# First expert's rows by products with 0/1 lists, second expert's by the gather, and an early choice for tiles 0 to 2

## The reference, cut to what matters

```
t = rms_norm(h, m_norm[layer])                       # (512, 1024)
g_logits = t @ w_group + b_group                     # 4 groups;  softmax, top 1
e_logits = t @ w_expert + b_expert                   # 16 experts, 4 to a group
# in the chosen group: top 2 of the 4 experts, weights from both softmaxes
for e in range(16):
    hdn = silu(t @ w_gate[e]) * (t @ w_up[e])        # 1024 -> 512
    y  += combine[:, e] * (hdn @ w_down[e])          # 512 -> 1024
h = h + y
```

## Time and profile before

| | |
|---|---|
| median of 3 runs | 1139.48 us (1138.67 to 1140.58) |
| the profiled execution | 1143.3 us, span 1141.5 us |
| TensorE busy | 1078.8 us (95%) |
| VectorE, ScalarE, GpSimd busy | 508.6, 282.6, 265.0 us |
| mean granted clock of TensorE | 0.980 |
| experts of layer 0, line 1843 | from 264.45 us |
| experts of layer 1, line 1843 | from 849.70 us |

### The profile page before, as it was taken

How to read it: one execution, slowest core, us unless ns; L and a number is a source line. 1 busy time by engine, 2 the same in 40 slices (tenths; PEclk the granted TensorE clock), 3 DMA queues, 4 the chain that set the end, 5 groups by cost and what they waited for, 6 DMA issues and landing times.

```text
span 1141.5 us, 17926 instructions
## 1 busy us (share of the span) xinstructions
PE 1078.8 (95%) x7469; PEld 647.0 (57%) x7469; DVE 508.6 (45%) x939; ACT 282.6 (25%) x461; POOL 265.0 (23%) x373
## 2 busy tenths in 40 slices
PE   6999999999999999996999999999989999999991
PEld 5688887874444433342788877777844444344430
DVE  3465237545533233326422357763355432343317
ACT  4442344320000000004232227763210000000012
POOL 1200012004333443123000013340023344433131
PEclk9899999999999999998999999999989999999996
DMA  9443311248999999998223210004279999999965
GB/s 322 127 146 112 106 38 74 110 186 331 402 422 421 422 423 423 423 418 288 102 75 111 79 69 1 2 1 166 71 263 415 419 421 421 422 423 423 423 230 198
DMA packets 68699, 283.24 MB, mean 248 GB/s; under 512 B 15048, under 2 KB 15216, under 8 KB 44064
## 3 DMA queue, kind: packets, MB, share of 16 engines
q1 hardware_dynamic: 47440, 239.32, 52.3%
q0 software_dynamic: 15232, 38.69, 9.4%
q10 hardware_dynamic: 5968, 4.40, 1.2%
HBM read 259.96 MB, written 22.41 MB: 247 GB/s over the span
## 4 chain that ended last, share of the span: by engine, by line
PE 81%; DVE 6%; DMA 4%; issue 4%; POOL 4%; ACT 1%; SPq 0%; POOLq 0%; DVEq 0%
PE ps L1843 41%; PE ps L1510 11%; PE ps L1512 10%; PE ps L1511 10%; DMA w_f<-in_m_w_up 2%; POOL xn_r L2295 1%; PE ps L1742 1%; DVE h L1384 1%; DMA xn<-output_table,pos 1%; PE ps L1520 1%; PE ps L1971 1%; DVE xn_r L1435 1%; POOL xn_r L2288 1%; PE ps L1654 1%; PE ps L1732 1%
## 5 line engine op out<-in xcount | busy, mean ns | idle before, releaser
L1843 PE MATMUL ps<-raw,s_f 128*32 128x256 f32 (+1 forms) x1536 | 175.8, 455 | 1.3 <-issue 0.7
L1843 PE MATMUL ps<-w_f,s_f 128*32 128x256 f32 (+1 forms) x1536 | 173.0, 451 | 2.6 <-issue 1.8
L1843 PE MATMUL ps<-xT_f,s_f 128*32 128x256 f32 (+1 forms) x1344 | 150.1, 451 | 0.4 <-DMA xT_f<-in_m_w_up 0.4
L1198 DVE TENSOR_TENSOR pad<-pad,ps 128x256 f32<-128x256 f32 x32 | 13.5, 421 | 296.6 <-ACT pad L790 296.6
L1843 PEld LDWEIGHTS ps<-raw,s_f 128*32 128x32 f32 (+1 forms) x1536 | 67.8, 119 | 103.5 <-issue 84.1
L1843 PEld LDWEIGHTS ps<-w_f,s_f 128*32 128x32 f32 (+1 forms) x1536 | 69.1, 119 | 95.4 <-issue 70.5
L1843 PEld LDWEIGHTS ps<-xT_f,s_f 128*32 128x32 f32 (+1 forms) x1344 | 59.7, 119 | 93.0 <-issue 74.0
L939 DVE SCALAR_TENSOR_TENSOR w_lo<-raw,gainT,w_hi 128x512 fp32r<-128x512 f32 x88 | 60.2, 746 | 105.3 <-ACT w_hi L594 105.3
L1208 DVE STREAM_TRANSPOSE s_f<-pad 32x128 f32<-32x128 f32 x256 | 103.0, 403 | 4.1
L1510 PE MATMUL ps<-w_hi,xT_hi 128*128 128x512 f32 x240 | 97.7, 407 | 5.9 <-DVE w_lo L939 2.9
L2252 POOL DMA_DIRECT2D output_table<-pad x60 | 33.7, 566 | 293.0 <-ACT pad L796 282.5
(11 more groups left out here) (299 smaller groups left out, 1470.8 us busy)
## 6 DMA issues: line engine op xcount, KB each, us to landing
raw<-in_m_w_down SPq DMA_DIRECT2D x28, 1024.0 KB
w_f<-in_m_w_down SPq DMA_DIRECT2D x28, 1024.0 KB
xT_f<-in_m_w_gate SPq DMA_DIRECT2D x26, 1024.0 KB
xT_f<-in_m_w_up SPq DMA_DIRECT2D x26, 1024.0 KB
raw<-in_m_w_gate SPq DMA_DIRECT2D x18, 1024.0 KB
raw<-in_m_w_up SPq DMA_DIRECT2D x18, 1024.0 KB
w_f<-in_m_w_gate SPq DMA_DIRECT2D x18, 1024.0 KB
w_f<-in_m_w_up SPq DMA_DIRECT2D x18, 1024.0 KB
```

Of the source, the lines that this page charges most:

```text
L1198: ve.tensor_tensor(hid2[:, 0:2 * P], sil2[:, 0:2 * P], ps[:, 0, 2 * P:4 * P], ALU.mult)
L1843: ins = te.matmul(ps[rows * n:rows * (n + 1), bank + kind, 0:width // parts], stationary(k, kind), weights(k, parts, n), start=k == 0, sto ...
```

## The change

It has four parts.

1. **Early choice.** The choice becomes a function `select(first, last)` of a range of tiles. VectorE does tiles 0 to 2 in `out_tiles`, between the logits of tile 2 and the last add; their ranks are multiplied by TensorE between the two halves of the last tile's logits. Tile 3 is chosen in `router`.
2. **First expert's rows by products.** From the ranks VectorE makes, for the first two experts only, 0/1 tables of token by row (`first_sel` in fp32, `second_sel` in bf16). TensorE multiplies `first_sel` by the normed rows in `xn`, eight products of 128x96 by 128x512 into two banks; VectorE and ScalarE copy a bank each to `x_0`, and TensorE transposes `x_0` as it did the gathered rows. `second_sel` is multiplied by the token numbers (eight products one column wide), and this list drives the whole-row gather, now of the second expert.
3. **What moves.** The lists of all experts, their transposition and the transposes of the second expert's rows are multiplied inside the first expert's `up`, which starts after the first half of its rows is copied. `overflow_places` stands ahead of `row_quarter_numbers` on VectorE. `x_first` is gone; `x_half` copies halves of either expert. The quarter gathers of the second expert are gone.
4. **The stream.** `load_down` of the first expert (pair 4) is issued ahead of the wait for the gather, which is now the second expert's. Pair 6, into `xn`, also waits for the first expert's wide products.

```
 class scratch:   -free = [6144]   +free = [11264]     (tables of the choice; the others stay at 6144)
+x_0 = pad[0:CAP, 0:D]
+index_1 = sb("index_1", [P, CAP])
+id_parts = sb("id_parts", [P, 2, NT], BF16)
...
 sync, load_pair:
                 if p == OWN:
                     sp.wait_ge(A["rows_stored"], 16 * NT * (layer + 1))
+                    sp.wait_ge(E["x_tr"], 6 * layer + 2)
 sync, step:
+                    load_down(layer, p + 2, e - 1, g)
                     if isinstance(e, int) and e == 1:
-                        sp.wait_ge(E["x_loaded0"], x_loads(layer, 0, -1))
-                    load_down(layer, p + 2, e - 1, g)
+                        sp.wait_ge(E["x_loaded1"], x_loads(layer, 1, -1))
...
 scalar, out_tiles:
                 rows_out(j)
+                act.wait_ge(E["x_tr"], 6 * layer + 2)
+                se.copy(x_0[:, BN:D], ps[0:CAP, 5, :]).then_inc(A["router_exp"], 1)
...
 vector:
+            def places_of(sel, e, first, last):
+                return tt(sel[:, first:last, :], index_1[:, :].unsqueeze(1).broadcast_to([P, last - first, CAP]),
+                          rank_of_first[:, first:last, e:e + 1].broadcast_to([P, last - first, CAP]), ALU.is_equal)
+            def ranks_in(layer, first, last):
+                dve.wait_ge(M["ranks_done"], 2 * layer + (1 if first == 0 else 2))
+                link(stt(rank_of_first[:, first:last, :], ps[:, 6, 0:NT * NE].rearrange("p (i e) -> p i e", e=NE)[:, first:last, 0:2], 1.0,
+                         sel_b[:, first:last, 0:2], ALU.add, ALU.mult))
 vector, out_tiles:
                 times_gain(0)
-                logits_in(j - 1)
+                link(logits_in(j - 1))
+                select(0, j)
                 add(j, 1)
+                ranks_in(layer, 0, j)
+                places_of(first_sel, 0, 0, j).then_inc(V["places_ready"], 1)
                 dve.wait_ge(M["hT_tr"], (NT + 1) * (layer + 1))
 vector, at the start, ahead of gainT's copy:
+            dve.wait_ge(G["consts"], 2)
+            ve.tensor_copy(id_parts[:, :, :], token_id[:, :, 0:NT])
 vector, router, ahead of the lists of all experts:
+                select(last, NT)
+                places_of(second_sel, 1, 0, last)
+                ranks_in(layer, last, NT)
+                places_of(first_sel, 0, last, NT).then_inc(V["places_ready"], 1)
+                places_of(second_sel, 1, last, NT).then_inc(V["places_ready"], 1)
+                dve.wait_ge(E["x_tr"], 6 * layer + 1)
+                ve.tensor_copy(x_0[:, 0:BN], ps[0:CAP, 4, :]).then_inc(V["places_ready"], 1)
...
+                dve.wait_ge(M["lists_done"], 4 * layer + 1)
+                ve.tensor_copy(token_now[:, 1:2], ps[0:CAP, 2, 2 * P:2 * P + 1]).then_inc(V["tokens_ready"], 1)
+                for f in (0, 1):
+                    x_half(layer, 0, f).then_inc(E["x_in"], 1)
 vector, experts:
+                overflow_places(layer)
                 row_quarter_numbers(layer)
-                x_first(layer)
-                overflow_places(layer)
+                x_half(layer, 1, 0)
+                x_half(layer, 1, 1).then_inc(E["x_in"], 1)
...
 tensor, out_proj:
                 logits(last, range(BK))
+                ranks(layer, range(last))
                 h_transposed_to(last, range(BK, KT))
+                pe.wait_ge(V["places_ready"], 6 * layer + 1)
+                pe.wait_ge(V["xn_ready"], NT * layer + last)
+                first_rows(0, 0)
                 logits(last, range(BK, KT))
+            def first_rows(t, n):
+                return te.matmul(ps[0:CAP, 4 + n, :], first_sel[:, t, :], xn[:, t, BN * n:BN * (n + 1)],
+                                 start=t == 0, stop=t == NT - 1, skip_group_check=True)
 tensor, router (kept_warm(3), the ranks of all tiles, kept_warm(1) and lists(...) go):
+                for t, n in ((0, 1), (1, 0), (1, 1), (2, 0), (2, 1)):
+                    first_rows(t, n)
+                ranks(layer, range(last, NT))
+                kept_warm(1)
+                pe.wait_ge(V["places_ready"], 6 * layer + 2)
+                pe.wait_ge(A["xn_scaled"], layer + 1)
+                for n in (0, 1):
+                    first_rows(last, n).then_inc(E["x_tr"], 1)
+                pe.wait_ge(V["places_ready"], 6 * layer + 3)
+                for t in range(NT):
+                    for c in range(2):
+                        ins = te.matmul(ps[0:CAP, 2, 2 * P:2 * P + 1], second_sel[:, t, :], id_parts[:, c, t:t + 1],
+                                        start=t + c == 0, stop=t + c == NT)
+                ins.then_inc(M["lists_done"], 1)
+                kept_warm(1)
+                pe.wait_ge(V["places_ready"], 6 * layer + 4)
+                pe.wait_ge(A["router_exp"], 3 * layer + 1)
+                x_transposed(E, x_0)
 tensor, experts (in up, the first callable stands behind the first four k blocks, the second behind the next four):
-                kept_warm(3)
-                x_transposed(E, layer, x_loads(layer, 0, -1))
-                up(I, 0, 0, 0, layer > 0)
+                def second_rows():
+                    pe.wait_ge(V["tokens_ready"], 4 * layer + 3)
+                    ...                                          (the transposed list, as before)
+                    pe.wait_ge(E["x_loaded1"], x_loads(layer, 1, -1))
+                    x_transposed(E, xg)
+                up(I, 0, 0, 0, layer > 0, (lambda: lists(6 * layer + 5, 7, NE), second_rows))
 gpsimd, experts:
-                gather(E, token[:, 0:1])
+                gather(token_now[:, 1:2], E["x_loaded1"])
                 pool.wait_ge(V["quads_ready"], layer + 1)
-                gather_quarters(1)
                 gather_quarters(2)
```

More of the change, by code:

```diff
@@ L217, in trunk @@
         gain_rows = pad[0:5 * KT, 13312:13312 + P]
-        free = [6144]
+        free = [11264]
         def scratch(*shape):
@@ L299, in x_loads, with x_ins @@
         def x_loads(layer, s, turn):
-            per_turn, own = 16 * GROUPS, 16 if s == 0 else 0
-            turns = NE // XG - (s == 0)
+            per_turn, own = 16 * GROUPS, 16 if s == 1 else 0
+            turns = NE // XG - (s < 2)
             return per_turn * turn + ((own + per_turn * turns + 32) * layer + own + per_turn)
         def outputs_loaded(layer, i):
-            return x_loads(layer, i, NE // XG - 1 - (i == 0)) + 32
+            return x_loads(layer, i, NE // XG - 1 - (i < 2)) + 32
+        def x_ins(layer, i):
+            return i + layer + 2
         O = [expert_sems(f"over{l}", "turn out_seen column column_seen x_hi x_lo h_tr h_hi h_lo") for l in range(LAYERS)]
@@ L1234, in last_list_out @@
                     ve.tensor_copy(last_rows, ps[0:CAP, 7, :]).then_inc(V["last_list"], 1)
-                step(I, 1, 0, 0, lambda: token_places(layer))
+                step(I, None, 0, 0, lambda: token_places(layer))
                 step(I + 1, 2, 0, 1, behind=lambda: token_weights(layer))
@@ L1241, in experts @@
                         s, ahead = (k + 2) % XG, (k + 2) // XG
-                        step(STEPS * g + (I + 1 + k), s, g + (ahead - (s == 0)), (k + 1) % 2)
+                        step(STEPS * g + (I + 1 + k), s, g + (ahead - (s < 2)), (k + 1) % 2)
                 step(I + NE - 1, None, 0, 1)
@@ L1790, in every, with ranks, x_transposed @@
                 return slice(k, k + n * (P - 1) + 1, n)
-            def x_transposed(S, i, loads):
-                pe.wait_ge(S["x_loaded0"], loads)
+            def first_rows(t, n):
+                return te.matmul(ps[0:CAP, 4 + n, :], first_sel[:, t, :], xn[:, t, BN * n:BN * (n + 1)],
+                                 start=t == 0, stop=t == NT - 1, skip_group_check=True)
+            def ranks(layer, tiles):
+                pe.wait_ge(V["sel_ready"], 2 * layer + (1 if tiles[0] == 0 else 2))
+                for i in tiles:
+                    o = ps[:, 6, NE * i:NE * (i + 1)]
+                    for j in range(i):
+                        te.matmul(o, ones_b[:, :], sel_b[:, j, :], start=j == 0, stop=False)
+                    ins = te.matmul(o, before[:, :], sel_b[:, i, :], start=i == 0, stop=True)
+                if tiles[-1] == NT - 1:
+                    o = ps[:, 6, NE * NT:NE * (NT + 1)]
+                    for j in range(NT):
+                        ins = te.matmul(o, ones_b[:, :], sel_b[:, j, :], start=j == 0, stop=j == NT - 1)
+                ins.then_inc(M["ranks_done"], 1)
+            def x_transposed(S, rows_in):
                 for f in (0, 1):
@@ L1846, in column_tiles, with up @@
                     return ins
-                def up(i, p, m, g=0, reuse=True):
-                    pe.wait_ge(E["x_in"], i + 1)
+                def up(i, p, m, g=0, reuse=True, behind=None):
+                    pe.wait_ge(E["x_in"], x_ins(layer, i) - (behind is not None))
                     if reuse:
@@ L1855, in up @@
                                 pe.wait_ge(*pair_of(layer, p + n, g))
+                                if n and behind is not None:
```

(3 more changed lines are left out.)

124 lines of the change are left out of this document (58 added, 66 removed).

## The result

The changed kernel takes 1143.69 us (median of 20 runs, 1136.44 to 1145.62), the kernel before, timed beside it, 1140.51 us (20 runs, 1137.88 to 1142.36). The ratio is 1.0022 with a 95% interval of 1.0012 to 1.0031: slower by some 0.2%, where 1133.3, some 0.5% faster, had been forecast. The profiled execution took 1145.36 us, span 1143.3.

What follows compares the result with a forecast made beforehand. TensorE's expert products bound the kernel, the weight stream close beside; the router ahead is pure path. Layer 0 -3.1, layer 1 -4.4, start +0.1 make -7.4; 1139.48 - 7.4 + 1.2 = 1133.3 us, range 1130.0 to 1138.5.

Steps and rivals of the forecast that it cites:

- (a) to (f): Layer 0's path from the early choice to the transposes: first expert starts at about 260.7, 3.8 us earlier than 264.45.
- What goes back: Lists and second expert's transposes inside the first up add some 1.9 us; it ends at 273.2 against 275.13.
- five rivals: Stream still binds (0.20), early choice or third rows late (0.11), half-clock stretch (0.12), clock stays half (0.05), no effect (0.05).
- signs of being wrong: A TensorE wait inside the first expert, the copy at 249.16 moving over 0.6, or a wait for weights.
- other signs: First expert 9.5 us after logits, its up 12.6, full clock, no gap above 0.5, last ranks 2.4 us late, stretch 238.0.
- the stretch of 238.0 us in both layers: Products from the second expert on last 238.0 us in each layer, against 239.20 and 238.05 before.
- rivals 3 and 4: Half clock on the router's wide products: a stretch in each layer, 1136.3 (0.12); from last logits to transposes, 1148.7 (0.05).
- The stream: Weight loads in layer 0 no longer fall behind the experts, so the 1.2 us lost to them is gained.
- The start: Copying the table of token numbers on VectorE ahead of the gains' copy costs 0.1 us, between 0 and 0.2.
- 1.2 of this for chance: Half of layer 1's 2.5 us from clock dips counted as not gained in timed runs, adding 1.2 to the forecast.
- -7.4: Sum over the profiled execution: -3.1 for layer 0, -4.4 for layer 1, +0.1 for the start.
- -4.4 forecast: Layer 1's first expert ends at 857.6 instead of 862.02; 2.5 us of the gain layer 1's own, mostly clock.

Runs made afterwards that it cites:

- e5: Changed kernel with the third expert's gathers issued behind the first expert's silu, not as soon as the row lists are there; 1143.91 us.
- e7: Kernel before with one wait added on GpSimd, so the third expert's gathers run while TensorE ends the first expert's up; 1142.90 us.
- e9: Changed kernel with number lists transposed earlier, inside the first kind of products, and quarter-row numbers written ahead of VectorE's overflow sums; 1136.48 us.
- e3: Changed kernel with one more 128x512 product in the pause ahead of the second expert's up, in both layers; 1140.03 us.
- e12: Changed kernel with the first expert's down weights loaded behind the wait for the gathered rows again, as before; 1144.05 us.
- e2: Changed kernel with only the second expert's eight transposes moved behind the first expert's up, the list products staying inside it; 1142.83 us.
- e1: Changed kernel with the second expert's row lists and transposes behind the first expert's up, not inside it; 1139.32 us.
- e6: e1 with the queue of loads not waiting for the second expert's gathered rows; 1141.14 us.
- e8: e5 with the queue of loads not waiting for the second expert's gathered rows; 1151.09 us.
- e4: Kernel before with only the load of the first expert's down weights moved ahead of the wait for the gathered rows; 1147.39 us.

## Why the prediction was wrong, step by step

- **The router, (a) to (f): right.** The choosing for three tiles ends 0.40 us before the last add (0.3 forecast); a wide product is two records some 0.44 apart (ten records in 4.36 us, 0.43 forecast); behind five of them, the last tile's ranks come 2.1 us after they could (2.4), the first expert 9.46 us behind the last logits (9.5 forecast). The clock is 1.00 there in both layers. The Trainium skill's rule that the forecast weighed, that activity releases the throttle ("TensorE: Matmul & The Clock Gate", "Part 1: The HAM clock gate"), would have it so, and here the trace agrees.
- **"What goes back": the failing step.** The sum of what stands inside the up was right (12.66 us from 261.70 to 274.36, 12.6 forecast). I followed the third expert's gathers only to the question whether their rows are in time, and called them hidden by 2 us; their issue at 271.7 was forecast to the tenth. What they lie beside I did not ask, and the sum put it at nothing without a reason. Before, six quarter-row gathers ran from 260.09 to 267.7, while TensorE did the products that keep its clock, transposed and did its first kind of products; the change leaves three of them and puts them 11.6 us later, from 271.68, over the 32-column products that end the up, and the silu learned of their end 1.7 us late, in each layer. e5, e7 and e9 show it. None of the five rivals is this one, and of the signs of being wrong none stood for it; of the other signs only the stretch of 238.0 us in both layers failed (239.07 and 239.51).
- **The clock.** I had looked for half clock on the router (rivals 3 and 4) and found none. It came at the second expert, 1.6 and 1.7 us, through the 2.56 us pause that the late silu makes; e3 removes it alone. Late silus and clock together are 2 x 1.69 + 1.57 + 1.69 = 6.6 us; e9 gives back 7.2 by its median.
- **The stream: right in size, by luck.** The stream waits of 1.7 us in layer 0 went (1.2 forecast), but they stay away without the reordered load too (e12), so the load is not the cause, and the reading that 14.2 us from the restart to the second expert were too few does not hold for the new kernels (12.2 and 12.9 us, with waits of 0.2 us at most). The cause is open.
- **The start.** The first gain product of VectorE came 0.9 us later in the trace (0.1 forecast), all but 0.1 of it in a wait for the small loads. The same start waits 0, 0, 0.3, 0.4, 0.65 and 1.24 us in the traces of e2, e3, e12, e9, e1 and e5: chance.
- **The base.** The trace of before lies 2.8 us above the median of 20 runs (1140.51). I took 1.2 of this for chance; e9, which has what the forecast describes, is 6.6 us under before in span and 3.8 in median. With all 2.8 taken for chance, the same -7.4 would have read 1140.5 - 7.4 + 2.8 = 1135.9.

The difference after minus before along the two traces: start +0.93, router and first expert -1.75, late silu +1.69, clock +1.57, stream -1.69: +0.75 at the last silu of layer 0. Between the layers +0.94 in GpSimd's stores of the table and +1.25 in half clock that lasts 13.6 us instead of 10.2; both vary (10.2 in e1's trace, 13.7 in e9's). Layer 1: router and first expert -4.13 (-4.3 counted from the last logits, -4.4 forecast), late silu +1.69, clock +1.69, a small rest of -0.4. End: +1.8, the difference of the spans.

## What to carry to other kernels

When a step moves, follow every instruction that it releases on the other queues and ask two questions of each: is it in time, and what does it now run beside. Here a train of gathers that was nowhere on the path cost 6 us by where it landed. A gain that is missing at the next hand-over between engines, with a releaser that the profile can't name, is a reason to set the update's own time beside the record of the instruction that made it.

## What the runs showed of the hardware

- While GpSimd issues indirect gathers, the completion of TensorE's 32-column products is seen late by the others, in 40 of 40 cases: one that ended in the single first gather was seen 0.31 us behind that gather's end (kernel before, line 1903), the last of the first up 0.84 to 1.03 us behind the end of the third gather of a train (changed kernel, e3, e7), that of the second up's first half 1.9 to 2.1 us behind the end of the ninth (e1 and e6 in layer 0, e5 and e8 in both). Transposes and 96-column list products that ended during a first gather were not late (e1: 0.01 us); those right behind a late 32-column product were (1.33 us in the changed kernel, up to 1.69 in e2). Whether the products are held or only their updates stays open: the changed kernel's records run on evenly, in e5 and e7 there are gaps between them.
- The Trainium skill, "Perfetto Trace Analysis", section "DMA Instruction — SWDGE (GPSIMD)", says that the end which the profile gives such an instruction is that of writing its descriptors, not of moving the data. The lateness beyond the last gather's end would fit with that; no run here shows whether it is the transfer.
- A pause of 2.5 to 2.6 us of TensorE between the first and the second expert was followed by half clock in both layers of the changed kernel and of e2, in layer 1 but not in layer 0 of e12, and not in layer 1 of e7; pauses of 0.91 and 1.60 us at this place were not (before, e1, e3, e5, e9). A stall of 1.80 us inside the first up was, in layer 0 of e8. Run by run the changed kernel's time follows its mean clock: 1136.44 us at 0.987, 1145.6 at 0.979.
- Loads of weights beside the rows slow both steps of the way to them. With the loads not held back, a whole-row gather takes 9.2 to 10.4 us from issue to landing (both layers of e6 and e8) instead of 4.0 to 4.6. With one pair loaded ahead (e4) the gather keeps its 4.3 to 4.6 us, but the store of the rows ahead of it ends later.
